# A decoder trunk on one core: when late weight units are split, and where the next part's first transposes stand

## The chip, the cores and the metric

The kernel runs on one core of one Trainium2 chip. The metric is the device time of one launch in microseconds (us), as the median of three runs. TensorE does the matmuls, ScalarE (ACT) and VectorE (DVE) prepare operands and take results out of PSUM, GpSimd (POOL) makes a few masks, and SyncE (SP) issues the weight loads.

## The reference, cut to what matters

The reference is a trunk of two layers over 512 tokens of width 1024. Each layer is four parts, and every part has the same frame:

```python
h = h + c * rmsnorm(part(rmsnorm(h, g_pre)), g_post)   # c = 1/2 for the feed-forward parts, else 1
# ffn:   (silu(x @ W_g) * (x @ W_u)) @ W_down           W_g, W_u: 1024 x 2816, W_down: 2816 x 1024
# even:  sparse attention heads and an RG-LRU, then @ W_out   (1024 x 1024)
# gla:   gated linear attention, then @ W_out                 (1024 x 1024)
# cross: softmax(q k^T) v over 256 memory tokens, then @ W_o  (1024 x 1024)
```

The eight parts in order are ffn (part 0), even (1), cross (2), ffn (3), ffn (4), gla (5), cross (6), ffn (7). So each part ends with a projection to width 1024, a norm over that width and an update of the residual `h`, and the next begins with a norm of `h`. Both norms need the whole row of a token.

## The kernel before, in words

**Split operands.** Every matmul of float32 data is made of three: each operand is split into a high part (the value copied to the fp32r type) and a low part (the difference), and high x high, high x low and low x high are summed. For a weight unit (128 x 1024 values, 512 KB) ScalarE makes the high part (`split_hi`, L299) and VectorE the low one (`split_lo`, L304) from `w_raw`, a buffer of two slots that SP loads in the order of the weight stream. SP may request unit v+2 only when VectorE's half of unit v is done. The units are split strictly in order on both engines, and four units ahead of use (`AHEAD`).

**Places of split units.** `w_hi` and `w_lo` have four places (`SLOTS`), used in turn. The last three units (`LATE`) of a part's output projection, where the next part is not a cross part, go to places of their own in `w_late`. This covers parts 0, 2, 3, 4, 6 and 7. `w_late` lies over the first activations of the ffn parts (`act_hi`): late unit n needs the bytes of the activations that units 2n and 2n+1 of a half read. `SLOT` and `LAST_USE` (L234 to L248) hold the place of each unit and the unit whose end makes the place free; `split_hi` waits for that end through `w_free`. For all three late units of an ffn part that is the sixth unit of the output's second half; in a cross part it is the last unit of the part's values, long past.

**The output projection** (`output` on three engines). The result has 1024 columns, made in two halves of 512 (`hf` 0 and 1), with 11 units a half in an ffn part and 4 in the others (`nu`). A unit takes 24 matmuls of 512 columns: four token tiles x two row blocks x three. Half 0 accumulates in PSUM banks 4 to 7, one for each token tile of 128, half 1 in banks 0 to 3. In half 1 the last three units are not taken unit by unit: TensorE goes tile by tile, and for each of the four tiles through the three late units (18 matmuls), so that tile 0 is done three tiles ahead of tile 3.

**The joint of two parts.** For each finished tile ScalarE squares half 1 with a row sum (`post_square`, L458), takes the root (L475), VectorE multiplies the half with the post gain (`store_half`, L1043), takes the reciprocal and updates `h` (L905); ScalarE squares the new `h` (L491) and takes a root, VectorE scales it to `f` (L923). TensorE then transposes `f` of the tile (`turn_x`, eight transposes, L1389) into banks 4 to 7; ScalarE copies the high part (`upper`, L500) and VectorE makes the low one (`lower`, L930). Before the change `turn_x` for tile 0 stands behind tile 2 of the late units and `turn_x` for tile 1 within tile 3, behind the second of its three late units. Then come the first half units of the next part, which need the first two tiles only (`half_unit`, L319 to L321 with 256 columns), and between them the turns of tiles 2 and 3.

**Orders written by hand.** In `output`, ScalarE and VectorE split one unit per step q of a half. The four squares of half 0 (ScalarE) and its four products (VectorE) stand ahead of the split in the last step of half 0. After the splits of half 1 (its steps end with the next part's first four units) ScalarE goes on to the squares of half 1, tile 0. The engine queues are in order, so a split that waits holds up every later instruction of that engine.

Of the kernel before, what the change touches and what calls it, by code (L numbers as in the profile page):

```python
# [9 lines left out]
KT = DM // P  # L10
TT = SEQ // P
# [16 lines left out]
LATE = 3  # L28
# [6 lines left out]
UNITS = {  # L35
    "ffn": [("gate_up", 2 * FT), ("down", FT)],
    "even": [("q_idx", 4), ("c_kv", 2), ("kw_idx", 1), ("x_b", 4), ("uk", 1), ("uv", 1), ("gate", 4), ("q", 4),
             ("out", KT)],
    "cross": [("k", KT), ("v", KT), ("q", KT), ("out", KT)],
    "gla": [("g_lr", 1), ("q", 4), ("k", 4), ("v", KT), ("r", KT), ("out", KT)],  # L40
}
# [9 lines left out]
def unit_starts(parts):  # L51

    at, n = {}, 0
    for i, (kind, _, _) in enumerate(parts):
        for seg, k in UNITS[kind]:
            at[i, seg] = n
            n += k
    return at, n


def trunk(nc, parts, x, mem, wstream, cols, gains, post_gains, mem_gains, head_gain, w_ra, w_ri, w_g2, out):
    f32, f32r = mybir.dt.float32, mybir.dt.float32r
    ALU, ACT, AX = mybir.AluOpType, mybir.ActivationFunctionType, mybir.AxisListType
    U, _ = unit_starts(parts)
    NU = wstream.shape[0]
    NP = len(parts)

    ctx = ExitStack()
    with ctx:
# [92 lines left out]
        def bank(b):  # L162
            return ps[:, b, :]
# [63 lines left out]
        def late_units(i):  # L227


            if i + 1 < NP and parts[i + 1][0] == "cross":  # L230
                return 0
            return LATE

        SLOT, LAST_USE, n = [], [], 0  # L234
        in_slot = {}
        for i, (kind, _, _) in enumerate(parts):
            for seg, k in UNITS[kind]:
                for q in range(k):
                    u = U[i, seg] + q
                    late = q - (k - late_units(i)) if seg in ("down", "out") else -1  # L240
                    if late >= 0:
                        SLOT.append(SLOTS + late)
                        LAST_USE.append(U[i, seg] + k // 2 + 2 * LATE - 1 if kind == "ffn" else U[i, "v"] + KT - 1)
                    else:
                        SLOT.append(n % SLOTS)
                        LAST_USE.append(in_slot.get(n % SLOTS))
                        in_slot[n % SLOTS] = u
                        n += 1  # L248

        def feeds_selection(i):  # L250


            return any(k == "even" for k, _, _ in parts[i:])

        def weights(u, at=slice(None)):

            s = SLOT[u]
            if s >= SLOTS:
                return w_late[:, 2 * (s - SLOTS), at], w_late[:, 2 * (s - SLOTS) + 1, at]
            return w_hi[:, s, at], w_lo[:, s, at]  # L260
# [9 lines left out]
        for i, (kind, _, _) in enumerate(parts):  # L270
            for seg, k in PROJ[kind].items():
                PT0[i, seg] = n
                n += k

        OUT = []
        for i, (kind, _, _) in enumerate(parts):
            seg, k = UNITS[kind][-1]
            OUT.append((U[i, seg], k // 2))

        def proj_bank(i, t):  # L280

# [159 lines left out]
        def _(act):  # L441
# [6 lines left out]
            def post_square(i, hf, t):  # L448

                u0, nu = OUT[i]  # L450
                if t < TT - 1:
# [127 lines left out]
            def mem_load(i):  # L579

                layer = parts[i + 1][1]
                if parts[i][0] == "even":
                    act.wait_ge(at_olo, O0[i] + AH // 2)
                else:
                    act.wait_ge(gs["y_ready"], 2 * TT)
                nc.scalar.dma_start(c_mem[:, :, :], mem.rearrange("(m p) d -> p m d", p=P)).then_inc(mem_in, 16)
                nc.scalar.dma_start(c_gain[:, :], mem_gains[layer:layer + 1, :].to_broadcast([P, DM]))\
                    .then_inc(mem_in, 16)
# [21 lines left out]
            def output(i, seg, nu):  # L610

                u0 = U[i, seg]
                mem_next = i + 1 < NP and parts[i + 1][0] == "cross"
                if mem_next:
                    mem_load(i)
                act.preload_act_table(ACT.Sqrt)

                if parts[i][0] == "ffn":
                    act.wait_ge(act_ready, (nffn[i] + 1) * FT + 2)
                nc.scalar.dma_start(tmp[:, 2:4, :].rearrange("p a b -> p (a b)"),  # L620
                                    post_gains[i:i + 1, :].to_broadcast([P, DM])).then_inc(post_in, 16)

                for hf in range(2):
                    for q in range(nu):
                        v = u0 + nu * hf + q + AHEAD
                        if hf == 0 and q == nu - 1:
                            for t in range(TT):
                                post_square(i, 0, t)
                        if v < NU:
                            split_hi(act, v)  # L630
                        if mem_next and q == 1:
                            mem_upper(i) if hf else mem_norm(i)
# [235 lines left out]
        def _(dve):  # L868
# [177 lines left out]
            def output(i, seg, nu):  # L1046

                u0 = U[i, seg]
                mem_next = i + 1 < NP and parts[i + 1][0] == "cross"
                for hf in range(2):  # L1050
                    for q in range(nu):
                        v = u0 + nu * hf + q + AHEAD
                        if hf == 0 and q == nu - 1:
                            half_sums(i)
                            for t in range(TT):
                                store_half(i, 0, t)
                        if v < NU:
                            split_lo(dve, v)
                        if mem_next and q == 1:
                            mem_lower(i) if hf else mem_norm(i)  # L1060
# [317 lines left out]
        def _(pe):  # L1378
# [3 lines left out]
            def turn_x(i, t):  # L1382

                pe.wait_ge(xs_ready, TT * i + t + 1)
                if t >= 2:
                    pe.wait_ge(x_ready, 2 * TT * i + 2 * (t - 2) + 2)
                for b in range(2):
                    for k in range(4):
                        last = nc.tensor.transpose(bank(4 + 2 * (t % 2) + b)[:, k * P:(k + 1) * P],  # L1389
                                                   f[:, t, (4 * b + k) * P:(4 * b + k + 1) * P], ident[:, :])  # L1390
                    last.then_inc(xT_ready, 1)
# [47 lines left out]
            def output(i, seg, nu, src_hi, src_lo):  # L1439

                u0, n0 = U[i, seg], nffn[i] * FT
                mem_next = i + 1 < NP and parts[i + 1][0] == "cross"

                def blocks(hf, q, t):
                    wh, wl = weights(u0 + hf * nu + q)
                    for j in range(2):
                        at = slice(j * SEQ, (j + 1) * SEQ)
                        ah, al = (a[:, 2 * q + j, t * P:(t + 1) * P] for a in (src_hi, src_lo))  # L1450
                        last = streamed(bank(4 - 4 * hf + t), ah, al, wh[:, at], wl[:, at],
                                        q + j == 0, q == nu - 1 and j == 1)
                    return last

                for hf in range(2):
                    late = late_units(i) if hf else 0
                    if parts[i][0] == "ffn":
                        pe.wait_ge(gu_free, hf * 2 + (n0 + FT))
                    for q in range(nu - late):
                        if parts[i][0] == "ffn":  # L1460
                            pe.wait_ge(act_ready, n0 + 2 * q + 4)
                        pe.wait_ge(w_ready, u0 + hf * nu + q + 1)
                        for t in range(TT):
                            last = blocks(hf, q, t)
                            if q == nu - 1 and t < TT - 1:
                                last.then_inc(o_full, 1)
                        last.then_inc(w_free, 1)
                        if q == 1 and mem_next and hf == 1:
                            mem_turn(i)
                    if late:  # L1470
                        pe.wait_ge(w_ready, u0 + (hf + 1) * nu)
                        for t in range(TT):
                            for q in range(nu - late, nu):
                                last = blocks(hf, q, t)
                                if t == TT - 1:
                                    last.then_inc(w_free, 1)
                                    if q == nu - 2 and i + 1 < NP:
                                        turn_x(i + 1, 1)
                            if t < TT - 1:
                                last.then_inc(o_full, 1)  # L1480
                            if t == TT - 2 and i + 1 < NP:
                                turn_x(i + 1, 0)

            def streamed(dst, ah, al, wh, wl, start, stop):

# [351 lines left out]
```

## Time and profile before

| | |
|---|---|
| median of 3 runs | 2469.28 us (2467.84 to 2470.05) |
| the profiled execution's own time | 2464.57 us |
| its span | 2462.0 us |
| TensorE busy (matmuls) | 2341.8 us, 95% |
| VectorE busy | 1037.7 us, 42% |
| ScalarE busy | 834.5 us, 34% |
| GpSimd busy | 47.9 us, 2% |
| loads | 221.81 MB, mean 90 GB/s |
| chain that ended last, by engine | TensorE 84%, VectorE 9%, issue 2%, DMA 2%, ScalarE 2% |

The span runs from the first to the last instruction of the profiled execution; its own time is 2.6 us longer. A matmul's row shows 0.39 us where the next one starts 0.23 us later, because matmuls overlap; the distance of starts is what a matmul costs. PEclk is the granted clock of TensorE as a share of 2.4 GHz. In a row of the timeline the bracket gives the idle time of the engine ahead of the instruction and what ended it; a row without a bracket followed directly.

### The profile page before, as it was taken

How to read it: one execution, taken by the hardware profiler on the slowest of the kernel's cores; microseconds unless marked ns; L12 is line 12 of the kernel's file. 1: busy time of each engine (PE TensorE's matmuls, PEld its weight loads, DVE VectorE, ACT ScalarE, POOL GpSimd, SP SyncE). 2: the span in 40 equal slices, each digit the busy share in tenths (PEclk: the TensorE clock that was granted, in tenths of full speed). 3: DMA queues.
4: the chain of work that ended last, by engine and by line, in shares of the span. 5: the costliest groups of instructions: out<-in, count | busy, mean ns of one | idle time of the engine just before them, and what ended most of it. 6: DMA issues, size and time to landing. Idle time of an engine off the chain costs nothing.

```text
span 2462.0 us, 28758 instructions
## 1 busy us (share of the span) xinstructions
PE 2341.8 (95%) x10808; PEld 1888.3 (77%) x10808; DVE 1037.7 (42%) x1608; ACT 834.5 (34%) x1311; POOL 47.9 (2%) x54
## 2 busy tenths in 40 slices
PE   7999998988899899999999999999989998999998
PEld 7888887563587588888888888887747866888887
DVE  4333235697562443333243333243364444433322
ACT  4222224353353343232233232244434433323221
POOL 0000000330000000000000000000000000000000
PEclk9999999796899999999999999999999999999999
DMA  4332332120134123333323333323203412233232
GB/s 155 98 97 94 110 104 82 40 74 16 60 112 128 37 70 108 98 98 102 97 77 108 97 99 103 96 83 98 86 26 111 146 60 77 77 100 96 94 103 85
DMA packets 61937, 221.81 MB, mean 90 GB/s; under 512 B 7952, under 2 KB 8080, under 8 KB 61856
## 3 DMA queue, kind: packets, MB, share of 16 engines
q1 hardware_dynamic: 57024, 207.64, 26.8%
q10 hardware_dynamic: 4832, 13.03, 1.5%
q8 instruction: 58, 0.95, 0.2%
q14 instruction: 23, 0.19, 0.0%
HBM read 218.55 MB, written 2.10 MB: 90 GB/s over the span
## 4 chain that ended last, share of the span: by engine, by line
PE 84%; DVE 9%; issue 2%; DMA 2%; ACT 2%; SPq 0%; DVEq 0%; ACTq 0%
PE ps L319 17%; PE ps L320 17%; PE ps L321 17%; PE ps L1486 9%; PE ps L1488 9%; PE ps L1487 9%; DMA w_raw<-in_wstream 2%; PE ps L1581 1%; DVE w_lo L304 1%; DVE e_sc L1204 1%; PE ps L1389 1%; DVE e_max L1203 1%; PE ps L1658 1%; PE ps L1617 1%; ACT w_hi L299 1%
## 5 line engine op out<-in xcount | busy, mean ns | idle before, releaser
L319 PE MATMUL ps<-x_hi,w_hi 128*128 128x512 f32 (+1 forms) x2016 | 749.8, 372 | 11.2 <-issue 9.0
L320 PE MATMUL ps<-x_lo,w_hi 128*128 128x512 f32 (+1 forms) x2016 | 747.1, 371 | 0.0
L321 PE MATMUL ps<-x_hi,w_lo 128*128 128x512 f32 (+1 forms) x2016 | 746.7, 370 | 0.0
L304 DVE TENSOR_TENSOR w_lo<-w_raw,w_hi 128x1024 fp32r<-128x1024 f32 x196 | 245.0, 1251 | 563.3 <-ACT w_hi L299 562.6
L319 PEld LDWEIGHTS ps<-x_hi,w_hi 128*128 128x128 f32 x2016 | 382.5, 190 | 79.7 <-issue 15.4
L321 PEld LDWEIGHTS ps<-x_hi,w_lo 128*128 128x128 f32 x2016 | 382.1, 190 | 64.7
L320 PEld LDWEIGHTS ps<-x_lo,w_hi 128*128 128x128 f32 x2016 | 382.5, 190 | 64.1 <-issue 0.2
L299 ACT ACTIVATE w_hi<-w_raw 128x1024 fp32r<-128x1024 f32 x196 | 207.2, 1057 | 405.7 <-PE ps L1488 314.9
L315 DVE TENSOR_TENSOR w_lo<-w_raw,w_hi 128x1024 fp32r<-128x1024 f32 x176 | 215.7, 1226 | 291.6 <-ACT w_hi L310 291.6
L310 ACT ACTIVATE w_hi<-w_raw 128x1024 fp32r<-128x1024 f32 x176 | 186.1, 1057 | 282.0 <-PE ps L321 275.4
L1486 PE MATMUL ps<-w_hi,act_hi 128*128 128x512 f32 x608 | 236.5, 389 | 0.0
L1487 PE MATMUL ps<-w_lo,act_hi 128*128 128x512 f32 x608 | 236.5, 389 | 0.0
L1488 PE MATMUL ps<-w_hi,act_lo 128*128 128x512 f32 x608 | 236.5, 389 | 0.0
L1008 DVE TENSOR_TENSOR tmp<-ps,tmp 128x512 f32<-128x512 f32 x88 | 60.8, 691 | 314.9 <-ACT tmp L572 314.9
L572 ACT ACTIVATE tmp<-ps 128x512 f32<-128x512 f32 x88 | 52.8, 600 | 369.9 <-PE ps L321 369.9
L1487 PEld LDWEIGHTS ps<-w_lo,act_hi 128*128 128x128 f32 x608 | 114.1, 188 | 23.9
L1488 PEld LDWEIGHTS ps<-w_hi,act_lo 128*128 128x128 f32 x608 | 114.1, 188 | 23.6
L1486 PEld LDWEIGHTS ps<-w_hi,act_hi 128*128 128x128 f32 x608 | 114.1, 188 | 23.6
L1486 PE MATMUL ps<-w_hi,x_hi 128*128 128x512 f32 x272 | 107.5, 395 | 8.8 <-DVE x_lo L1360 4.5
L1487 PE MATMUL ps<-w_lo,x_hi 128*128 128x512 f32 x272 | 106.8, 393 | 0.0
L1488 PE MATMUL ps<-w_hi,x_lo 128*128 128x512 f32 x272 | 106.7, 392 | 0.0
L1389 PE MATMUL ps<-ident,f 128*128 128x128 f32 x256 | 38.2, 299 | 32.0 <-DVE f L923 32.0
(263 smaller groups left out, 2200.2 us busy)
## 6 DMA issues: line engine op xcount, KB each, us to landing
w_raw<-in_wstream SPq DMA_DIRECT2D x390, 512.0 KB, 3.6
gain_bc<-in_gains ACTq DMA_DIRECT2D x8, 512.0 KB, 4.3
tmp<-in_post_gains ACTq DMA_DIRECT2D x8, 512.0 KB, 4.4
c_mem<-in_mem ACTq DMA_DIRECT2D x2, 1024.0 KB, 5.4
out_dram<-h SPq DMA_DIRECT2D x4, 512.0 KB, 2.6
h<-in_x SPq DMA_DIRECT2D x2, 512.0 KB, 6.2
h<-in_x ACTq DMA_DIRECT2D x2, 512.0 KB, 7.5
c_gain<-in_mem_gains ACTq DMA_DIRECT2D x2, 512.0 KB, 6.7
```

The costliest lines, as they stand in the source:

```text
L299: nc.scalar.activation(weights(v)[0], w_raw[:, v % 2, :], ACT.Copy).then_inc(w_hi_ready, 1)
L304: nc.vector.tensor_tensor(wl, w_raw[:, v % 2, :], wh.bitcast(f32), ALU.subtract).then_inc(w_ready, 1)
L310: nc.scalar.activation(weights(like)[0], w_raw[:, like % 2, :], ACT.Copy).then_inc(w_hi_ready, 1)
L315: nc.vector.tensor_tensor(wl, w_raw[:, like % 2, :], wh.bitcast(f32), ALU.subtract).then_inc(w_ready, 1)
L319: nc.tensor.matmul(dst, wh, xh, start=start, stop=False)
L320: nc.tensor.matmul(dst, wh, xl, start=False, stop=False)
L321: return nc.tensor.matmul(dst, wl, xh, start=False, stop=stop)
L1008: nc.vector.tensor_tensor(tmp[:, jj, :], bank(2 * jj + 1), tmp[:, jj, :], ALU.mult)\
L1389: last = nc.tensor.transpose(bank(4 + 2 * (t % 2) + b)[:, k * P:(k + 1) * P], f[:, t, (4 * b + k) * P:(4 * b + k + 1) * P], ident[:, :])
L1486: nc.tensor.matmul(dst, ah, wh, start=start, stop=False)
L1487: nc.tensor.matmul(dst, ah, wl, start=False, stop=False)
L1488: return nc.tensor.matmul(dst, al, wh, start=False, stop=stop)
```

## The change

Four things are changed. (1) A late unit of an ffn part waits for its own place: late unit n for unit 2n+1 of the second half, instead of unit 5 for all. (2) In parts whose half has at most `LATE + 1` units and which have late units (the cross parts 2 and 6), the squares and products of half 0 move from step (0, nu - 1) to step (1, 2). (3) `turn_x` of tile 0 moves from behind tile 2 to tile 3, behind the second of its late units. (4) `turn_x` of tile 1 moves from there to behind the third. `OUT` moves up in the code because the new function reads it. In the diff the first changed condition is ScalarE's, the second VectorE's, and the last piece is TensorE's loop over the late units.

```diff
-                        LAST_USE.append(U[i, seg] + k // 2 + 2 * LATE - 1 if kind == "ffn" else U[i, "v"] + KT - 1)
+                        LAST_USE.append(U[i, seg] + k // 2 + 2 * late + 1 if kind == "ffn" else U[i, "v"] + KT - 1)
...
+        def first_half_read(i):
+            nu = OUT[i][1]
+            return (1, 2) if nu <= LATE + 1 and late_units(i) else (0, nu - 1)
...
-                        if hf == 0 and q == nu - 1:
+                        if (hf, q) == first_half_read(i):
                             for t in range(TT):
                                 post_square(i, 0, t)
...
-                        if hf == 0 and q == nu - 1:
+                        if (hf, q) == first_half_read(i):
                             half_sums(i)
                             for t in range(TT):
                                 store_half(i, 0, t)
...
                                 if t == TT - 1:
                                     last.then_inc(w_free, 1)
                                     if q == nu - 2 and i + 1 < NP:
-                                        turn_x(i + 1, 1)
+                                        turn_x(i + 1, 0)
                             if t < TT - 1:
                                 last.then_inc(o_full, 1)
-                            if t == TT - 2 and i + 1 < NP:
-                                turn_x(i + 1, 0)
+                        if i + 1 < NP:
+                            turn_x(i + 1, 1)
```

## Rows read from the trace of the kernel before

**Rows 1.** The page: TensorE's busy time, and two of the costliest groups

```profile
PE 2341.8 (95%) x10808; PEld 1888.3 (77%) x10808; DVE 1037.7 (42%) x1608; ACT 834.5 (34%) x1311; POOL 47.9 (2%) x54
...
L304 DVE TENSOR_TENSOR w_lo<-w_raw,w_hi 128x1024 fp32r<-128x1024 f32 x196 | 245.0, 1251 | 563.3 <-ACT w_hi L299 562.6
...
L1389 PE MATMUL ps<-ident,f 128*128 128x128 f32 x256 | 38.2, 299 | 32.0 <-DVE f L923 32.0
```

**Rows 2.** Timeline of TensorE, joint 3→4: start, length, instruction [idle before, releaser]

```profile
1260.25 0.39 PE L1488 MATMUL ps<-w_late,act_lo 128*128 128x512 f32 x1
1264.61 1.97 PE L1389 MATMUL ps<-ident,f 128*128 128x128 f32 x8 [3.97 <-DVE f L923]
...
1269.63 1.09 PE L1389 MATMUL ps<-ident,f 128*128 128x128 f32 x8
...
1271.95 0.28 PE L319 MATMUL ps<-x_hi,w_hi 128*128 128x256 f32 x1
```

**Rows 3.** Timeline of TensorE, turns 0 and 1 of the other four joints

```profile
377.64 1.09 PE L1389 MATMUL ps<-ident,f 128*128 128x128 f32 x8 [2.98 <-DVE f L923]
...
383.18 1.09 PE L1389 MATMUL ps<-ident,f 128*128 128x128 f32 x8 [1.70 <-DVE f L923]
...
894.48 1.97 PE L1389 MATMUL ps<-ident,f 128*128 128x128 f32 x8 [4.87 <-DVE f L923]
...
900.21 1.04 PE L1389 MATMUL ps<-ident,f 128*128 128x128 f32 x8
...
1632.81 1.97 PE L1389 MATMUL ps<-ident,f 128*128 128x128 f32 x8 [2.69 <-DVE f L923]
...
1638.05 1.04 PE L1389 MATMUL ps<-ident,f 128*128 128x128 f32 x8
...
2085.94 1.34 PE L1389 MATMUL ps<-ident,f 128*128 128x128 f32 x8 [4.08 <-DVE f L923]
...
2091.23 1.04 PE L1389 MATMUL ps<-ident,f 128*128 128x128 f32 x8
```

**Rows 4.** Timeline of ScalarE, joint 3→4: splits, and the square of tile 0

```profile
1226.74 1.06 ACT L299 ACTIVATE w_hi<-w_raw 128x1024 fp32r<-128x1024 f32 x1 [4.38 <-PE ps L1488]
1237.62 2.01 ACT L299 ACTIVATE w_late<-w_raw 128x1024 fp32r<-128x1024 f32 x2 [9.82 <-PE ps L1488]
...
1258.19 0.58 ACT L458 ACTIVATE tmp<-ps 128x512 f32<-128x512 f32 x1
```

**Rows 5.** Chain of waits in time, joint 3→4: start, length, what (weight loads)

```profile
1240.11 3.39 DMA w_raw<-in_wstream
...
1246.02 5.01 DMA w_raw<-in_wstream
```

**Rows 6.** Timeline of VectorE, joint 3→4: scaling and the low part of x

```profile
1268.29 1.29 DVE L923 SCALAR_TENSOR_TENSOR f<-h,stat,gain_bc 128x1024 f32<-128x1024 f32 x1
...
1270.96 1.29 DVE L930 TENSOR_TENSOR x_lo<-ps,x_hi 128x512 fp32r<-128x512 f32 x2 [0.18 <-ACT x_hi L500]
...
1276.33 1.29 DVE L923 SCALAR_TENSOR_TENSOR f<-h,stat,gain_bc 128x1024 f32<-128x1024 f32 x1
```

**Rows 7.** Timeline of ScalarE (three) and VectorE (one), joint 2→3

```profile
861.70 1.06 ACT L299 ACTIVATE w_late<-w_raw 128x1024 fp32r<-128x1024 f32 x1 [3.98 <-DMA w_raw<-in_wstream]
...
872.55 1.05 ACT L299 ACTIVATE w_late<-w_raw 128x1024 fp32r<-128x1024 f32 x1
...
887.09 1.06 ACT L299 ACTIVATE w_hi<-w_raw 128x1024 fp32r<-128x1024 f32 x1 [3.81 <-DMA w_raw<-in_wstream]
...
872.77 2.48 DVE L1043 TENSOR_TENSOR f<-ps,tmp 128x512 f32<-128x512 f32 x4
```

**Rows 8.** Timeline of ScalarE, joint 0→1: the square of tile 0

```profile
370.70 0.58 ACT L458 ACTIVATE tmp<-ps 128x512 f32<-128x512 f32 x1
```

**Rows 9.** A matmul released by x_lo; window 894:896 (last: PEclk, DMA share, GB/s)

```profile
849.86 0.50 PE L1486 MATMUL ps<-w_hi,x_hi 128*128 128x512 f32 x1 [1.41 <-DVE x_lo L1079]
...
894.00:896.00 2.00, 1.52 (x7) 1.52 (x8) 1.97 (x4) 0.00 (x0) 0.00 (x0) 0.50 0.00 0
```

More of the change, by code:

```diff
@@ L232, in late_units @@
             return LATE
+        OUT = []
+        for i, (kind, _, _) in enumerate(parts):
+            seg, k = UNITS[kind][-1]
+            OUT.append((U[i, seg], k // 2))
         SLOT, LAST_USE, n = [], [], 0
@@ L273, in trunk @@
                 n += k
[L275 to L278, printed above, removed]
         def proj_bank(i, t):
```

## The prediction

> **What bounds the kernel now.** I read the page first: TensorE is busy 95% of the span, so only its idle and slowed stretches can be won [rows 1]. In the table of costly groups the transposes of L1389 (the turns) stand out: 32.0 us idle before them, released by VectorE's `f` of L923 [rows 1]. Next comes TensorE's timeline around each boundary between two parts. I call them joints: five have late units (0→1, 2→3, 3→4, 4→5, 6→7). In joint 3→4 the third token tile's last matmul ends at 1260.64 (1260.25 + 0.39), then TensorE stands 3.97 us until turn 0 starts at 1264.61 [rows 2]. The others stand 2.98 and 1.70 (0→1, before both turns), 4.87, 2.69 and 4.08 us [rows 3]; with 3.97 that is 20.3 of the 32.0. The rest is the start of the kernel and one later turn, which the change leaves.
>
> The waits cost more than their length. In four joints turn 0 lasts 1.3 to 2.0 us against 1.04 to 1.09 us for turn 1 [rows 2, 3], and the granted clock over 894 to 896 is 0.50, the lower level of 1.2 GHz [rows 9]. From start to start of the two turns I count 5.02 us (3→4), 5.73 (2→3), 5.24 (4→5), 5.29 (6→7) [rows 2, 3]. At 2.4 GHz it would be 3.68: a turn and six matmuls take 2.32 (1269.63 to 1271.95 [rows 2]), and six more at a pitch of 0.227 (two units of 24 matmuls in 10.88 us [rows 4]) take 1.36. So the low clock costs 1.34 to 2.05 us a joint on top.
>
> Why is `f` late? ScalarE's timeline: its split of the first late unit waits 9.82 us to 1237.62, two units (2 x 5.44) behind the split before it at 1226.74, because all three late units wait for the sixth unit of the second half [rows 4]. Seven splits then run as fast as loads land: requests of 3.39 to 5.01 us in two buffers [rows 5]. The square of tile 0 starts with no idle before it, at 1258.19 [rows 4]; its result had been there since 1260.64 - 8.16 = 1252.48 (two tiles of 18 matmuls, 4.08 each). ScalarE is 5.7 us behind, and the whole chain square, mean, update, square, scale, turn with it.
>
> **Part by part: the late units' own places.** In ffn parts late unit 0 may now be split when the second unit of the half is done, late 1 with the fourth, late 2 with the sixth. No instruction is added. Joint 3→4 with the same durations (split 1.06 on ScalarE, 1.25 on VectorE, then the request) [rows 1, 4, 5]: late 0 follows its forerunner at 1227.7. Late 1's load is requested at 1229.1 and lands at 1232.5 to 1234.1. Late 2 keeps its gate, 1237.6. The next part's four follow, the first from about 1239. The last is requested at the latest at 1247.4, if all loads take 5.01, lands at 1252.4 and ends on ScalarE at 1253.5; with loads near 3.5 it ends at 1251. Its gate is the end of the eighth unit, 1248.4. So the square of tile 0 starts at 1252.5 to 1253.5; I take 1252.5, as a load in this stretch shares the queue with one other at most.
>
> `f` of tile 1 ended 1269.58 (1268.29 + 1.29), 11.39 behind the square of tile 0 [rows 4, 6]: new 1263.9 to 1264.9.
>
> **The turns.** Turn 0 now stands behind two late units of the last tile, turn 1 behind the third. TensorE, not standing: slot end of tile 2 at 1260.48, 12 matmuls 2.72, turn 0 at 1263.20, turn 0 and six matmuls 2.32, turn 1 at 1265.52. `f` of tile 0 (some 5 us ahead of `f` of tile 1) and of tile 1 are there, with 0.6 to 1.6 us to spare. Turn 1 moves from 1269.63 to 1265.52: 4.11 us.
>
> What is late next: behind turn 1 nothing covers the way to the next part's first half unit. VectorE's first difference starts 1.33 behind the turn's start (1270.96 against 1269.63), one takes 0.64 (two in 1.29), and a matmul that `x_lo` releases, as the one at 849.86, I let follow after 0.05 [rows 2, 6, 9]. So the half unit starts 2.0 behind turn 1's start instead of 2.32, and TensorE stands 1.2 us. That bubble is new, yet costs nothing net, for it takes the place in which the last six matmuls stood, now ahead of the turn. Its bounds: 0.3 us gain as computed, or 1 us loss if ScalarE, which has the square of tile 2 (0.8 us) between the two copies, is late; by the chain above it is free 0.7 us ahead, so I take neither. Turn 2 needs `f` of tile 2, which ended 1277.62 [rows 6], behind VectorE's work on tiles 1 to 3 that starts with the difference behind turn 1. It moves with turn 1, by 4.11, and TensorE will wait about 0.3 us for it. So each joint gains what turn 1 moves.
>
> **The other joints**, by the same formula: new turn 1 = (turn 0's old start - its idle - 0.16) + 5.04 [rows 3].
> - 0→1: 374.50 + 5.04 = 379.54, from 383.18: 3.64 us. Here the chain is longer, and turn 1 itself waited for `f`; the square started at 370.70 and can start at 366.5 [rows 8], so `f` of tile 1 comes at about 378.9, 0.6 us to spare.
> - 2→3: 889.45 + 5.04 = 894.49, from 900.21: 5.72.
> - 4→5: 1629.96 + 5.04 = 1635.00, from 1638.05: 3.05.
> - 6→7: 2081.70 + 5.04 = 2086.74, from 2091.23: 4.49.
>
> **The squares of the first half** move in the two cross parts, where each output half has four units, from ahead of the last late unit's split to ahead of the next part's third. By the code that is three splits passed on ScalarE and on VectorE, not two. In 2→3 the last late split starts 872.55, behind four squares, though the one before it was at 861.70; the last of all starts 887.09 [rows 7]. Moved, that late split goes as its load lands (about 864), the next two by 868 and 871, then four squares (0.58 each, I take 0.8 with what lies between) to 875 [rows 4], VectorE's four products (2.48 us) to 878 [rows 7], the third split by 876 and 879, and the fourth at its gate: the end of the half's first unit, 889.45 - 12.25 = 877.2, so by 878.5 and 880.2. The square of tile 0 is free at 881.45: ScalarE is 3 us early. For the same at loads of 5.01 us the margin is some 1 to 2 us. If the squares had stayed, the last late split would still hold up the next ones, so this edit carries the 5.72 and 4.49 us of its joints.
>
> At the last part (7) late units are split earlier, and nothing waits for that: 0. SP's load requests come earlier, none is added. POOL has no step here.
>
> **The sum**: 3.64 + 5.72 + 4.11 + 3.05 + 4.49 = 21.0 us. The profiled execution took 2464.57 (span 2462.0), so 2443.6 (span 2441.0). The median of the three runs is 2469.28, 4.7 above that execution; 2469.28 - 21.0 = 2448.3 is my number.
>
> **Rivals.** (a) *Loads are the bound.* The seven splits do not get ahead, ScalarE reaches tile 0 as late as now, and the turns only move. Then turn 1 waits for `f` of tile 1, which comes 5.02 behind that of tile 0 (joint 3→4, where it just did not stand), against 5.73, 5.24 and 5.29 from turn to turn now: 0.7, 0.2 and 0.3 us of gain in three joints, nothing in the others, 2468.1. For it: the chain now runs through loads [rows 5]. Against: ScalarE stood 9.82 us with a loaded unit at hand [rows 4], time for two loads.
>
> (b) *The clock falls in the new bubbles.* Waiting is cut from one stretch into a turn, six matmuls, a turn and 1.2 us of standing. If TensorE goes to 1.2 GHz there, each joint pays about what the low clock costs now, 1.34 to 2.05 us: 7 to 10 us over five, 2455 to 2459. For it: 2.69 us of standing sufficed in 4→5. Against: 2.98 and 1.70 us in 0→1 did not, both turns there lasted 1.09 [rows 3]. The Trainium skill ("TensorE: Matmul & The Clock Gate", "A second HAM failure mode: psum-queue depth-cycling") says that small idle gaps between groups of matmuls, met often enough, can make the clock swing; by it these five joints would come out at (b)'s time. Joint 0→1 is the one place of this trace with such short gaps, and does not show it.
>
> (c) *Slower: the wait comes together behind the last late unit.* As in (a) the splits stay late, and the wait, now between turn 0 and turn 1 and ahead of wide work, lowers the clock over the first half units: each joint pays 1.34 to 2.05 us plus the slow turn, 0.9 (1.97 against 1.09 [rows 2, 3]); I take 1.9 in all: 2468.1 + 5 x 1.9 = 2477.6. It decides from the point where `f` of tile 1 comes over 2.7 us behind the third late unit's end. Needs (a) first.
>
> **Chances.** Forecast 0.72, (b) 0.12, (a) 0.07, (c) 0.03, and 0.06 for a partial gain between forecast and (a), loads near 5 us everywhere. The forecast's own bounds: up to 2.7 us more if VectorE reaches tile 0 0.5 us earlier and turn 2 does not wait, 5 us less if each joint loses 1 us in the bubble: 2445.6 to 2453.3. With (b) inside, the range is 2444 to 2459. A change under 0.2% (4.9 us) can't be told from none: faster than 2464.3 holds the forecast, (b) and most of the partial case, 0.90; within 0.07; slower 0.03.
>
> **What would show it.** Right: idle before turn 0 near zero in all five joints; turns of about 1.1 us everywhere; a new idle of about 1.2 us before L319 of the next part, released by `x_lo`; ScalarE's square of tile 0 waiting for TensorE instead of starting with no idle; a granted clock of 1.00 around 895. Wrong: an idle before turn 1 released by `f` means (a); a turn of 1.6 us or more, or half units at double pitch, means (b) or (c). An idle before the late units released by a split in the cross parts would mean that the moved squares were not what held them.

## The result and the profile after

The changed kernel takes 2444.35 us (median of five runs, 2441.76 to 2449.96), against 2467.84 for the kernel before in the same comparison (2466.50 to 2470.05). The ratio is 0.9905, with a 95% interval of 0.9891 to 0.9920: 0.95% faster, 23.5 us between the medians. The forecast was 21.0 us and 2448.3. The measured time is 4.0 us under that: inside the stated range of 2444 to 2459, but only just, and 1.3 us outside the forecast's own bounds of 2445.6 to 2453.3. Of the 4.0 us, 1.4 come from the base (2469.28 was the median of three runs, 2467.84 that of the five here); the rest is taken up below.

The page of the profile after: the span, the busy times, the chain that ended last. (Lines of the kernel file are 6 higher than before.)

```profile
span 2442.6 us, 28758 instructions
...
PE 2337.8 (96%) x10808; PEld 1884.9 (77%) x10808; DVE 1038.6 (43%) x1608; ACT 835.6 (34%) x1311; POOL 48.0 (2%) x54
...
PE 89%; DVE 7%; issue 2%; ACT 1%; DMA 0%; SPq 0%; DVEq 0%; ACTq 0%
```

Instruction counts are the same as before [rows 1]. TensorE's busy time fell by 4.0 us: in the joints the turns of tiles 0 and 1 last 1.03 us, and none of them runs at 1.2 GHz any more. The chain had 2% of loads in it before, in front of the joints; now the only load in it is the one at the start of the kernel.

TensorE's timeline in joint 3→4 (start, length, instruction, idle before), to be laid beside [rows 2]:

```profile
1256.41 1.03 PE L1395 MATMUL ps<-ident,f 128*128 128x128 f32 x8
...
1258.66 1.03 PE L1395 MATMUL ps<-ident,f 128*128 128x128 f32 x8
...
1260.76 0.36 PE L325 MATMUL ps<-x_hi,w_hi 128*128 128x256 f32 x1 [1.07 <-DVE x_lo L936]
...
1266.64 1.09 PE L1395 MATMUL ps<-ident,f 128*128 128x128 f32 x8
```

The idle of 3.97 us before turn 0 is gone, both turns last 1.03 us, and one new idle stands ahead of the first half unit: 1.07 us, released by `x_lo`. Joint 0→1 looks the same, and turn 2 still waits there:

```profile
378.63 1.03 PE L1395 MATMUL ps<-ident,f 128*128 128x128 f32 x8
...
380.89 1.03 PE L1395 MATMUL ps<-ident,f 128*128 128x128 f32 x8
...
382.99 0.35 PE L325 MATMUL ps<-x_hi,w_hi 128*128 128x256 f32 x1 [1.07 <-DVE x_lo L936]
...
390.15 1.09 PE L1395 MATMUL ps<-ident,f 128*128 128x128 f32 x8 [1.18 <-DVE f L929]
```

To compare joints across kernels I measure from one mark that no edit moves: the slot end of tile 2 (the start of the matmul that would follow it). Where turn 0 stands behind tile 2 and no idle is before it, the mark is turn 0's start; where it waited, its start less the idle and 0.16; where turn 0 stands two late units later, 2.72 us less. Turn 2, the first instruction that waits for `f` of tile 2, is where a joint's gain is read. (The forecast column is the gain of turn 1, which the prediction took for the joint's.) Distances from the mark, in us, before from [rows 2, 3] and turn 2 of the same timeline:

| joint | turn 1 before | after | turn 2 before | after | gain | forecast |
|---|---|---|---|---|---|---|
| 0→1 | 8.68 | 4.98 | 18.01 | 14.24 | 3.8 | 3.64 |
| 2→3 | 10.76 | 4.98 | 18.76 | 12.96 | 5.8 | 5.72 |
| 3→4 | 9.15 | 4.97 | 17.22 | 12.95 | 4.3 | 4.11 |
| 4→5 | 8.09 | 4.98 | 16.09 | 12.96 | 3.1 | 3.05 |
| 6→7 | 9.53 | 4.97 | 17.53 | 12.96 | 4.6 | 4.49 |
| sum | | | 87.6 | 66.1 | 21.5 | 21.0 |

The spans differ by 19.4 us, the profiled executions by 20.2, the medians by 23.5, and the joints by 21.5. The rest lies between the joints, and most of it varies from trace to trace: the mark of joint 0→1 stands at 375.91 after and at 374.50 before (374.4 to 377.0 in all traces of this case), and the stretch from there to joint 2→3, behind turn 2, takes 498.3 after and 496.9 before, but 497.4 in a second trace of the changed kernel. The two stretches between joints 2→3, 3→4 and 4→5 take 352.2 to 352.3 in every trace but one (352.5 in e3 below). The five runs of the changed kernel spread over 8 us. So 21.5 us is the change's gain in the joints; that the 2.0 us more between the medians is of the change is not shown.

ScalarE in joint 3→4, to be laid beside [rows 4]: the splits, and the square of tile 0.

```profile
1219.94 1.06 ACT L305 ACTIVATE w_hi<-w_raw 128x1024 fp32r<-128x1024 f32 x1 [4.38 <-PE ps L1494]
1220.90 1.04 ACT L305 ACTIVATE w_late<-w_raw 128x1024 fp32r<-128x1024 f32 x1
1225.89 1.06 ACT L305 ACTIVATE w_late<-w_raw 128x1024 fp32r<-128x1024 f32 x1 [3.95 <-DMA w_raw<-in_wstream]
1230.82 1.06 ACT L305 ACTIVATE w_late<-w_raw 128x1024 fp32r<-128x1024 f32 x1 [3.86 <-PE ps L1494]
...
1244.01 1.06 ACT L305 ACTIVATE w_hi<-w_raw 128x1024 fp32r<-128x1024 f32 x1 [3.95 <-DMA w_raw<-in_wstream]
1245.72 0.60 ACT L464 ACTIVATE tmp<-ps 128x512 f32<-128x512 f32 x1 [0.65 <-PE ps L1494]
```

The three late units are split 0.96, 5.95 and 10.88 us behind the split before them (forecast 1, about 6 to 7, 10.9), and the square of tile 0 now waits 0.65 us for TensorE instead of following the last split. `f` of tile 1 and of tile 2 on VectorE, beside [rows 6]:

```profile
1255.29 1.29 DVE L929 SCALAR_TENSOR_TENSOR f<-h,stat,gain_bc 128x1024 f32<-128x1024 f32 x1
...
1265.30 1.28 DVE L929 SCALAR_TENSOR_TENSOR f<-h,stat,gain_bc 128x1024 f32<-128x1024 f32 x1
```

`f` of tile 1 is done at 1256.58. Turn 1 takes it at 1258.66, 2.1 us later: there was more to spare than the 0.6 to 1.6 us that I had counted. `f` of tile 2 is done at 1266.58, and turn 2 starts at 1266.64: that is the bound now. The wait itself is short: from the first half unit to turn 2 it is 5.88 us, where it was 5.75 before, so 0.13 us against the 0.3 forecast.

Joint 2→3 on ScalarE, beside [rows 7]: the last late split, the third of the splits that went ahead of the squares, the first square, the two splits behind them, the square of late tile 0.

```profile
862.88 1.06 ACT L305 ACTIVATE w_late<-w_raw 128x1024 fp32r<-128x1024 f32 x1 [1.24 <-DMA w_raw<-in_wstream]
...
869.26 1.06 ACT L305 ACTIVATE w_hi<-w_raw 128x1024 fp32r<-128x1024 f32 x1 [1.64 <-DMA w_raw<-in_wstream]
870.23 0.58 ACT L464 ACTIVATE tmp<-ps 128x512 f32<-128x512 f32 x1
...
873.13 1.05 ACT L305 ACTIVATE w_hi<-w_raw 128x1024 fp32r<-128x1024 f32 x1
876.45 1.06 ACT L305 ACTIVATE w_hi<-w_raw 128x1024 fp32r<-128x1024 f32 x1 [2.26 <-PE ps L1494]
880.47 0.60 ACT L464 ACTIVATE tmp<-ps 128x512 f32<-128x512 f32 x1 [2.96 <-PE ps L1494]
```

ScalarE stands 2.96 us before late tile 0, where 3 was forecast. The granted clock (third number from the right) around the bubble of joint 3→4 stays at 1.00. It is 1.00 in the first 2 us of half units of the other four joints as well, so rival (b) did not come about:

```profile
1260.00:1262.00 2.00, 1.24 (x10) 1.27 (x11) 1.96 (x5) 1.43 (x5) 0.00 (x0) 1.00 0.00 0
```

### The profile page after: what moved, and what is told of

It is laid out like the page before. It is cut to its first block, busy times and chain, and to the rows that moved or that the text cites. A ratio compares the mean times of both kernels' runs of the same rounds, so it can differ in the third digit from the quotient of the medians.

```text
span 2442.6 us, 28758 instructions
## 1 busy us (share of the span) xinstructions
PE 2337.8 (96%) x10808; PEld 1884.9 (77%) x10808; DVE 1038.6 (43%) x1608; ACT 835.6 (34%) x1311; POOL 48.0 (2%) x54
## 4 chain that ended last, share of the span: by engine, by line
PE 89%; DVE 7%; issue 2%; ACT 1%; DMA 0%; SPq 0%; DVEq 0%; ACTq 0%
PE ps L325 17%; PE ps L327 17%; PE ps L326 17%; PE ps L1492 10%; PE ps L1494 10%; PE ps L1493 10%; PE ps L1587 1%; DVE e_sc L1210 1%; DVE e_max L1209 1%; PE ps L1664 1%; PE ps L1395 1%; DVE w_lo L310 1%; PE ps L1623 1%; PE ps L1578 1%; PE ps L1656 0%
## 5 line engine op out<-in xcount | busy, mean ns | idle before, releaser
L325 PE MATMUL ps<-x_hi,w_hi 128*128 128x512 f32 (+1 forms) x2016 | 750.9, 372 | 16.2 <-issue 8.6
L325 PEld LDWEIGHTS ps<-x_hi,w_hi 128*128 128x128 f32 x2016 | 382.8, 190 | 85.2 <-issue 21.5
L1492 PEld LDWEIGHTS ps<-w_hi,x_hi 128*128 128x128 f32 x272 | 51.6, 190 | 21.6 <-DVE x_lo L1085 6.1
```

Source lines behind the costliest of these rows:

```text
L325: nc.tensor.matmul(dst, wh, xh, start=start, stop=False)
L1492: nc.tensor.matmul(dst, ah, wh, start=start, stop=False)
```

## The experiments

The question left by the result: the prediction took the change as a whole. Which edit brings the gain, and did the turns have to move? Theory S, formed from the spare 2.1 us above: the late splits and the squares were the whole hold-up, and once `f` is early the old places of the turns are the better ones. Rival T: the turns had to move for `f` to be ready.

The kernels e1, e2 and e3 each make one part of the change in the kernel before.

### e1: the late units' own places alone

```diff
-  ... U[i, seg] + k // 2 + 2 * LATE - 1 if kind == "ffn" ...
+  ... U[i, seg] + k // 2 + 2 * late + 1 if kind == "ffn" ...
```

> The kernel before with the late units' own places alone; the squares of the first half and both turns stay where they were. Theory S (the late splits held ScalarE up; once the scaled f is early, the old places of the turns are the better ones): only the joints behind ffn parts gain (0 to 1, 3 to 4, 4 to 5). There f of tile 0 is ready before tile 2 ends (2.1 us before, by the changed kernel's trace) and f of tile 1 about 2.8 us behind it, ahead of the 3.6 us at which the old place of turn 1 comes. Turn 2, which sets the pace of what follows, then starts 11.7 us behind the end of tile 2 instead of 17.2 (3 to 4) and 16.1 (4 to 5), and about 13.5 instead of 18.0 in joint 0 to 1: 5.5 + 4.4 + 4.5 = 14.4 us, so 2453.4. Theory T (the turns had to move for f to be ready in time): f comes late at the old places and the joints gain at most what the changed kernel shows there, 3.8 + 4.3 + 3.1 = 11.2 us, so 2456.6 or more, with idle before turn 1. The joints behind the cross parts stay as before (idle of 4 to 5 us before turn 0).

Measured: 2455.41 us beside 2468.11 for the kernel before, ratio 0.9946 (0.9928 to 0.9964). The span is 2453.4. TensorE in joint 3→4:

```profile
1261.27 1.03 PE L1389 MATMUL ps<-ident,f 128*128 128x128 f32 x8
...
1264.88 1.03 PE L1389 MATMUL ps<-ident,f 128*128 128x128 f32 x8
...
1272.89 1.07 PE L1389 MATMUL ps<-ident,f 128*128 128x128 f32 x8
```

No idle in this joint, turn 1 at 3.61 and turn 2 at 11.62 behind the mark. The joints behind ffn parts gain 4.7 + 5.6 + 4.5 = 14.8 us, those behind cross parts stay at idle of 4.09 and 4.01 us before turn 0. That is S. The median moved by 12.7, between S's 14.4 and T's 11.2, and cannot tell them apart; the trace decides.

### e2: the squares and products of half 0 alone

```diff
-                        if hf == 0 and q == nu - 1:
+                        if (hf, q) == first_half_read(i):
```

The same condition is changed for VectorE's products, and the new function comes with it.

> The kernel before with the first half's squares and products of the cross parts moved alone. Theory S: only joints 2 to 3 and 6 to 7 gain, turn 2 from 18.8 and 17.5 us behind the end of tile 2 to 11.7: 7.1 + 5.8 = 12.9 us, so 2454.9. Theory T: at most 5.8 + 4.6 = 10.4 us, so 2457.4. A third view, that the late units' waits were the whole hold-up and the squares did not matter: 2467.8, no change. The joints behind ffn parts as before.

Measured: 2451.91 us, ratio 0.9942 (0.9924 to 0.9959), 16.2 us under the kernel before. Turn 2 stands at 11.63 and 11.64 us in the two cross joints (7.1 + 5.9 = 13.0 us); the other three keep an idle of 3.04, 3.71 and 2.63 us before turn 0. The third view falls: in the cross parts the squares and products of half 0 held the split of the last late unit and those behind it. The two moved together, on ScalarE and on VectorE; no run tells which of them held the splits. The median fell by 3.3 us more than S says, and the joints by what S says (13.0 against 12.9).

### e3: the turns alone

```diff
                                     if q == nu - 2 and i + 1 < NP:
-                                        turn_x(i + 1, 1)
+                                        turn_x(i + 1, 0)
...
-                            if t == TT - 2 and i + 1 < NP:
-                                turn_x(i + 1, 0)
+                        if i + 1 < NP:
+                            turn_x(i + 1, 1)
```

> The kernel before with the two turns moved alone. The splits stay late, so f of tile 1 comes when it did and turn 1 waits for it. Rival (a) of the prediction as a kernel: 0 to 0.7 us gained in each of five joints, 2466.6, no change that can be told. Rival (c): the wait between the turns and the bubble behind them lowers the clock over the first half units, 1.9 us a joint more: 2476, with turns of 1.6 us or more and half units at double distance. Idle before turn 1 of some 2.7 us in joint 3 to 4 (f at the old time, turn at 1265.5 if free), released by f.

Measured: 2472.60 us over eleven runs, ratio 1.0016 (1.0005 to 1.0027): slower by about 4 us. Neither number of the expectation was met: it lies between (a) and (c), and what the trace shows is (c)'s. Joint 2→3, TensorE's turn 1 and first half-unit matmuls, then the granted clock:

```profile
900.32 1.82 PE L1389 MATMUL ps<-ident,f 128*128 128x128 f32 x8 [2.53 <-DVE f L923]
902.80 0.55 PE L319 MATMUL ps<-x_hi,w_hi 128*128 128x256 f32 x1 [0.65 <-DVE x_lo L930]
...
903.58 0.41 PE L319 MATMUL ps<-x_hi,w_hi 128*128 128x256 f32 x1
903.79 0.41 PE L320 MATMUL ps<-x_lo,w_hi 128*128 128x256 f32 x1
```

```profile
902.00:904.00 2.00, 1.35 (x6) 1.23 (x6) 1.84 (x3) 1.65 (x5) 0.00 (x0) 0.50 0.00 0
```

TensorE stands 2.53 us for `f` of tile 1 and then again for `x_lo`, and the half units start at 1.2 GHz: 0.21 us from start to start, where 0.12 is their pace at full clock. In all five joints the way from the first half unit to turn 2 takes 7.3 to 8.4 us, where it takes 5.9 in four joints of the changed kernel; the turns themselves were slow in two joints only (1.55 and 1.82 us). Turn 2 comes 18.9, 19.5, 19.1, 17.2 and 18.5 us behind the mark, 5.5 us later in sum than before. So the turns' new places, with the splits still late, are a loss.

### e4 and f2: the changed kernel with both turns at their old places

Its edit is e3's, backwards, on the changed kernel.

> The changed kernel with both turns back at their old places (tile 0 behind tile 2 of the late units, tile 1 behind the second late unit of tile 3). Theory S: 14.4 + 12.9 = 27.3 us under the kernel before, 2440.5, that is 4 us faster than the changed kernel: turn 1 comes 3.6 us behind the end of tile 2 instead of 5.0, the last late unit again covers the way from turn 1 to the next part's half unit, and the bubble of 1.07 us is gone in all joints; turn 2 at 11.7 us instead of 13.0. Theory T: no faster than the changed kernel, 2444.4 or slower, with idle before a turn released by f.

> The changed kernel with both turns at their old places once more. By the distance from the end of tile 2 to turn 2 in the two traces (13.3 against 14.2 us in joint 0 to 1, 11.6 against 13.0 in the four others) it is 6.3 us faster than the changed kernel of this call. If the 5 us seen between the calls were drift, no difference.

Measured: 2439.14 us (2437.93 to 2441.72) against 2468.11, ratio 0.9884 (0.9864 to 0.9903); in the second comparison 2441.51 (2439.22 to 2442.69) against 2467.66, ratio 0.9895 (0.9880 to 0.9910).

```profile
1252.84 1.03 PE L1395 MATMUL ps<-ident,f 128*128 128x128 f32 x8
...
1256.46 1.03 PE L1395 MATMUL ps<-ident,f 128*128 128x128 f32 x8
...
1264.46 1.07 PE L1395 MATMUL ps<-ident,f 128*128 128x128 f32 x8
```

Four joints have no idle at all on TensorE, with turn 2 at 11.6 us; joint 0→1 keeps 0.22 and 1.09 us of waiting for `f` of tiles 1 and 2 (turn 2 at 13.3). The sum over the joints is 59.8 us, against 66.1 of the changed kernel and 87.6 before. S is met, T is not.

### f1: the changed kernel once more

> The changed kernel once more, so that it stands on the same chip and beside the same runs of the kernel before as the three below. All theories: 23 us under the kernel before in this call.

Measured: 2443.55 us (2441.74 to 2447.53), ratio 0.9903 (0.9888 to 0.9918), 24.1 us under. Against f2 in this comparison 2.0 us, not 6.3. Over all comparisons the nine runs of the changed kernel average 2444.5 and the eight with the old turns 2440.4: 4.1 us. The sum over the joints was 66.1 and 59.8 in each of the two traces of either kernel, 6.3 us apart, but the spans of these traces differ by 3.5 and 4.6 only: the stretch of parts 1 and 2 took 1.4 and 0.9 us longer with the old turns, and that of parts 5 and 6 1.4 and 0.7. What varies there is told at the end; whether a faster joint gives some of its gain back in these parts, or chance does, stays open. On the clock the old places are worth 2 to 5 us by the medians.

### f3 and f4: which turn's place counts

Both are edits of the changed kernel. f3 has turn 0 behind tile 2 and turn 1 behind the last late unit; f4, whose edit is shown, has both behind the second late unit of tile 3:

```diff
                                     if q == nu - 2 and i + 1 < NP:
                                         turn_x(i + 1, 0)
+                                        turn_x(i + 1, 1)
...
-                        if i + 1 < NP:
-                            turn_x(i + 1, 1)
```

> The changed kernel with turn 0 back behind tile 2 and turn 1 left behind the last late unit. Theory P (the place of turn 1 alone sets the pace, because VectorE's difference behind it opens the work that ends in f of tile 2): turn 1 stays 5.0 us behind the end of tile 2, so the same time as the changed kernel within 1 us, with the bubble of 1.07 us. Rival B (each turn that stands late costs its share): half of the difference comes back, 3 us faster than the changed kernel.

> The changed kernel with turn 0 where it stands there (behind the second late unit of tile 3) and turn 1 right behind it, ahead of the third. Theory P: turn 1 comes 3.6 us behind the end of tile 2, no bubble, and the time is that of the kernel with both turns at their old places, 6 us faster than the changed kernel (0.1 to 0.4 us of idle for f of tile 1 may be left in joint 0 to 1). Rival B: 3 us faster only.

f3 measured 2446.84 us (ratio 0.9916, 0.9902 to 0.9929) and has the changed kernel's joints to within 0.02 us: turn 1 at 4.98, a bubble of 1.07, turn 2 at 12.96 (14.25 in joint 0→1), sum 66.1. The two spans are equal as well, 2441.8. By the medians f3 is 3.3 us slower than f1, which nothing in the joints explains. So turn 0's place is free, and rival B falls.

f4 measured 2443.51 us (ratio 0.9903, 0.9888 to 0.9918), no faster than the changed kernel by the median, and its joints sum to 62.6: turn 1 is early as expected, but 0.37 us of bubble are left in four joints, and turn 2 stands at 12.3, not 11.6 (13.5 in joint 0→1). ScalarE's timeline tells why: with the turns back to back the square of tile 2 lies between the two copies, and the second copy starts when the square ends, 4.9 us behind the mark. In e4 the first copy and the square are done before turn 1, and the second copy starts 4.25 us behind the mark. The 0.64 us between them are what turn 2 loses.

```profile
1257.78 1.09 ACT L506 ACTIVATE x_hi<-ps 128x512 fp32r<-128x512 f32 x2 [1.98 <-PE ps L1395]
1258.75 0.61 ACT L464 ACTIVATE tmp<-ps 128x512 f32<-128x512 f32 x1
1259.23 0.21 ACT L464 ACTIVATION_READ_ACCUMULATOR tmp<-ps 128x1 f32 x1
1259.32 1.10 ACT L506 ACTIVATE x_hi<-ps 128x512 fp32r<-128x512 f32 x2
```

Theory P needs that correction: what sets the pace is the copy and difference behind turn 1, which the turn's place bounds only while ScalarE is free.

### g1: only late unit 0 has its own wait

The three g kernels are edits of e4 and ask how much of each part is needed. e4 itself did not run beside them; it is compared by its ratio to the kernel before (0.9884) and by its trace.

```diff
-  ... U[i, seg] + k // 2 + 2 * late + 1 if kind == "ffn" ...
+  ... U[i, seg] + k // 2 + (1 if late == 0 else 5) if kind == "ffn" ...
```

> The kernel with both turns at their old places, but in ffn parts only late unit 0 has its own wait (second unit of the half), late 1 and 2 both wait for the sixth again. Theory L (what counts is that the chain of loads is ahead of ScalarE by the end of late tile 0, and one unit let go early is nearly enough): late 1 and 2 are split at the sixth unit's end, both loaded by then, the last of the next part's four about 1 to 1.5 us later than now, ScalarE is free within 0.5 us of the end of late tile 0, and f of tile 1 has 0.8 us to spare: 0 to 2 us slower than the kernel with all three waits. Rival M (each late unit's own place carries a third of the ffn joints' 14.7 us): 5 to 10 us slower, with idle before turn 0 or 1 in joints 0 to 1, 3 to 4 and 4 to 5.

Measured: 2440.26 us beside 2470.18, ratio 0.9881 (0.9864 to 0.9898), the same as with all three waits within what runs tell. In the trace it costs: turn 2 at 14.9, 12.7 and 12.6 in the ffn joints instead of 13.3, 11.6 and 11.6, 3.5 us in sum, more than L's 0 to 2 and less than M's 5 to 10, so neither expectation was met. The idle before turn 1 that M named is there: 1.67, 0.86 and 0.71 us. The last splits and the square of tile 0 in joint 3→4:

```profile
1244.43 1.06 ACT L305 ACTIVATE w_hi<-w_raw 128x1024 fp32r<-128x1024 f32 x1 [4.75 <-DMA w_raw<-in_wstream]
1245.68 1.06 ACT L305 ACTIVATE w_hi<-w_raw 128x1024 fp32r<-128x1024 f32 x1 [0.19 <-DMA w_raw<-in_wstream]
1246.65 0.58 ACT L464 ACTIVATE tmp<-ps 128x512 f32<-128x512 f32 x1
```

ScalarE is late again, by about 1.2 us (the last split starts 7.8 us ahead of the mark at 1253.47, in the changed kernel 9.7). So the first unit let go carries 11.2 of the 14.8 us, and late units 1 and 2 the rest.

### g2 and g3: the squares behind one split, and behind two

```diff
-            return (1, 2) if nu <= LATE + 1 and late_units(i) else (0, nu - 1)
+            return (1, 0) if nu <= LATE + 1 and late_units(i) else (0, nu - 1)   # g3: (1, 1)
```

> The kernel with both turns at their old places, but in the cross parts the first half's squares stand at step (1, 0): behind one split (the last late unit's) instead of three. Theory L: the next part's first split waits for the squares until 1.3 us behind the first half's end, VectorE's four products lie ahead of its half, the loads behind them come late, and ScalarE is some 3 us late for late tile 0: 2 to 3 us in each of two joints, 4 to 6 us slower. Rival N (it is only the last late unit that must go ahead of the squares): no difference.

> The same with the squares at step (1, 1), behind two splits. Theory L: the second of the next part's splits is 2.6 us later on ScalarE and 4 us on VectorE, its successor's load lands 3 us later, about when late tile 0 ends: 0 to 1 us slower in all, no idle before turn 1 or at most some tenths. Rival N: no difference. That the third split passed is needed: 4 us slower or more.

g2 measured 2440.95 us (ratio 0.9880, 0.9862 to 0.9897), g3 2441.86 (0.9883, 0.9866 to 0.9900): by the medians neither differs from e4. In the traces g2's two cross joints have turn 2 at 13.1 and 13.0, 2.8 us in sum, with an idle of 1.15 and 1.13 before turn 1; g3's stand at 11.65 and 11.62, no loss. L's direction and place hold for both, but for g2 its size was too high, 4 to 6 us against 2.8: the square of tile 0 started 1.5 and 1.4 us behind the end of tile 0 where L had some 3, and turn 1 came 1.4 and 1.3 us late. By the trace two splits ahead of the squares do as well as three.

## Why the prediction was right

- **Late splits hold ScalarE, and `f` with it**: shown. e1 and e2 take the cause away at three and at two joints, and the idle before turn 0 goes there and nowhere else. Loads took 3.4 to 4.7 us ahead of joint 3→4, as assumed, and the last split ended 0.65 us ahead of late tile 0; I had it between 1.5 us ahead and 1 us behind.
- **The low clock's share** of 1.34 to 2.05 us in four joints came back: turns of 1.03 us, clock 1.00, busy time 4.0 us less.
- **Turn 1 at 5.04 behind the mark**: 4.97 to 4.98.
- **The bubble** of 1.2 us: 1.07, in all five joints, without a fall of the clock. Rival (b) is out for this kernel. In e3 the clock did fall over the half units in all five joints (granted 0.50 to 0.66 in 2 us of each): there TensorE stood 2.5 to 3.1 us, did a turn and stood 0.65 to 1.07 us more. Two things in the prediction were too sure. It let (c) begin where `f` comes over 2.7 us late; in e3 2.53 us of standing, with the bubble behind it, were enough. And it called joint 0→1 the one place of the trace with short gaps, which is not so: in part 2 TensorE stands 0.95, 0.35 and 1.42 us within 4 us, and there the clock does fall in most traces (last section). The weight put against (b) rested on less than the text says.
- **"So each joint gains what turn 1 moves"**: turn 1 moves by 3.70, 5.78, 4.18, 3.11 and 4.56, turn 2 gains 3.8, 5.8, 4.3, 3.1, 4.6, against 3.64, 5.72, 4.11, 3.05, 4.49.
- **"This edit carries" the cross joints' gain**: shown by e2; e1 shows the same of the places for the ffn joints.
- **What the prediction did not see**: it called the bubble free, since it "takes the place in which the last six matmuls stood". Against the kernel before that holds, and the sum is right by it. Against the turns' old place with an early `f` it is not free: turn 1 stands 1.36 us later than it could. The prediction never put that kernel beside its own, and so did not see that edits (3) and (4) take back 6.3 of 27.8 us in the joints. The rows for it were there: `f` of tile 1 follows the square of tile 0 by 11.39 us, which with the early square put it 3.4 us behind the mark at best (2.9 in the trace after), ahead of the 3.6 us of the old turn 1.

- **Luck**: the joints give 21.5 us for 21.0. That the median came out 4.0 us under the forecast is the base (1.4), the joints (0.5) and 2.0 us that no trace accounts for. The range's lower end is 0.35 us away, far less than launches spread, and two of the five runs lie under it.

Rival (c) was priced at 1.9 us a joint on top of (a), which lies 1.2 us under the kernel before. e3's joints are 5.5 us over it, so (c) cost 6.7 us over five joints, 1.3 a joint.

## What to carry to other kernels

When a wait is removed, look at every placement that was chosen around that wait: here the turns stood best where they were, and moving them took back more than a fifth of the gain in the joints. Judge each part of a change by a mark in the trace that no part moves; differences of 2 to 4 us, clear there to hundredths, were lost in a spread of 2 to 15 us between the launches of one kernel. Then look at what lies between the marks too: there 6.3 us in the joints had become 3.5 and 4.6 us of span. And on an in-order engine, put the work whose result is due late (the first half's squares) behind the work that starts a chain of loads.

## What the runs showed of the hardware

The clock fell to 1.2 GHz after 2.69 us of standing in joint 4→5 [rows 3], but not after 2.98 and 1.70 us in joint 0→1 [rows 3], nor after the 1.07 us bubbles of the changed kernel, f1 and f3; in e2 joint 0→1 it fell after a wait of nearly the same length, 3.04 us (turn 0 there lasted 1.76 us, the granted clock over 378 to 381 was 0.75). Equal waits end at either level from one trace to the next. The eight matmuls of 512 columns in part 2 that follow waits of 0.95, 0.35 and 1.42 us show it best. First e2, where the granted clock stayed at 1.00 (845 to 849), then g3, where it was 0.50 (842 to 846):

```profile
845.89 3.70 PE L1587 MATMUL ps<-c_pT,c_v 128*128 128x512 f32 x8 [1.42 <-DVE c_pT L1116]
```

```profile
841.48 6.64 PE L1587 MATMUL ps<-c_pT,c_v 128*128 128x512 f32 x8 [1.42 <-DVE c_pT L1116]
```

They took 3.7 us in e2 and f3, 5.4 in the kernel before, in both traces of the changed kernel, in e3 and in f2, and 6.6 to 6.7 in e1, e4, g1, g2 and g3. These 3 us are more than half of what the stretch of parts 1 and 2 varies by.

Ahead of the joints, loads of 512 KB took 3.3 to 5.3 us in the traces looked at. In joint 3→4 before, the loads requested at 1223.8 and 1229.2, with no other weight load in flight, took 3.4 us each, and the pair requested at 1246.0 and 1248.2, which overlapped, 5.0 and 4.3.
